# A hybrid decoder step on one core: fifteen of the low parts of the expert rows move from VectorE to GpSimd in each layer

## What is computed

```python
q = (h @ wq).reshape(T, PEER_HEADS, 2, PEER_KDIM // 2)
s = jnp.einsum('thpc,hpkc->thpk', q, subkeys)
s_top, i_top = lax.top_k(s, 16)
cand = s_top[:, :, 0, :, None] + s_top[:, :, 1, None, :]
cs, ci = lax.top_k(cand.reshape(T, PEER_HEADS, 256), 16)
g = jax.nn.softmax(cs, axis=-1)
act = jax.nn.gelu(jnp.einsum('td,thkd->thk', h, u[e]), approximate=False)
out = jnp.einsum('thk,thkd->td', g * act, v[e])
```

## Time and profile before

| What | Value |
|---|---|
| Median of 3 runs | 2259.3 us (2253.72 to 2259.88) |
| Profiled execution: its time | 2260.83 us |
| Its span | 2259.0 us |
| TensorE clock granted, mean | 0.99 |
| Busy: PE, DVE, ACT, POOL | 2180.9, 1562.3, 1281.5, 107.9 us |
| u tiles 0 to 64, first layer | 340 to 535 us of the span |
| u tiles 0 to 64, second layer | 1451 to 1646 us |

### The profile page before, as it was taken

The page is one execution under the profiler, slowest core; times in us unless marked ns, Lnnn a source line. Parts: engine busy times, 40 slices in busy tenths (PEclk is TensorE's granted clock), DMA queues, the critical chain, the costliest instruction groups (busy, mean ns, idle before and its releaser), DMA issues.

```text
span 2259.0 us, 39872 instructions
## 1 busy us (share of the span) xinstructions
PE 2180.9 (97%) x15478; PEld 1844.6 (82%) x15478; DVE 1562.3 (69%) x3318; ACT 1281.5 (57%) x2439; POOL 107.9 (5%) x140
## 2 busy tenths in 40 slices
PE   5999999999999999999999999999999999999998
PEld 3566599999999877778865667999999998777786
DVE  2375469896889877666634754798878897675666
ACT  1254345657888755565513544356588886555654
POOL 1200010000000000000021000100000000001000
PEclk9999999999999999999999999999999999999999
DMA  8342516776565688876563433277765657888564
GB/s 262 135 150 77 201 52 245 263 263 238 199 230 204 230 314 311 309 244 216 178 217 139 145 113 131 100 276 265 256 230 200 227 203 255 310 295 313 186 195 150
DMA packets 143320, 481.67 MB, mean 213 GB/s; under 512 B 25698, under 2 KB 52384, under 8 KB 139022
## 3 DMA queue, kind: packets, MB, share of 16 engines
q1 hardware_dynamic: 132638, 438.71, 56.1%
q0 software_dynamic: 10496, 40.42, 5.0%
HBM read 475.81 MB, written 104.21 MB: 257 GB/s over the span
## 4 chain that ended last, share of the span: by engine, by line
PE 81%; DVE 9%; DMA 6%; SPq 2%; ACT 1%; issue 1%; DVEq 0%; ACTq 0%
PE ps L1140 27%; PE ps L1098 26%; PE ps L806 8%; PE ps L1109 5%; DMA region<-in_peer_v 3%; PE ps L771 3%; DVE parts_low L1976 2%; PE ps L1059 1%; PE ps L1067 1%; PE ps L1063 1%; DMA region<-in_peer_uT 1%; PE ps L796 1%; DMA big<-in_state_win_k 1%; PE ps L815 1%; DVE big L1898 1%
## 5 line engine op out<-in xcount | busy, mean ns | idle before, releaser
L1976 DVE TENSOR_TENSOR parts_low<-region,parts_high 128x1024 fp32r<-128x1024 f32 x512 | 625.7, 1223 | 352.1 <-ACT parts_high L1358 350.3
L1358 ACT CAST parts_high<-region 128x1024 fp32r<-128x1024 f32 x512 | 537.8, 1051 | 307.0 <-PE ps L1140 195.3
L1140 PE MATMUL ps<-parts_high,parts_hw 128*128 128x512 f32 x2048 | 640.0, 392 | 17.3 <-DVE parts_low L1976 11.7
L1098 PE MATMUL ps<-tokens_hi,parts_high 128*128 128x256 f32 x2048 | 590.1, 288 | 14.7 <-DVE parts_low L1976 14.6
L1098 PE MATMUL ps<-tokens_hi,parts_low 128*128 128x256 f32 x2048 | 575.0, 281 | 0.0
L1098 PE MATMUL ps<-parts_hw,parts_high 128*128 128x256 f32 x2048 | 575.0, 281 | 0.0
L1140 PEld LDWEIGHTS ps<-parts_high,parts_hw 128*128 128x128 f32 x2048 | 386.6, 189 | 108.9 <-issue 16.1
L1098 PEld LDWEIGHTS ps<-tokens_hi,parts_high 128*128 128x128 f32 x2048 | 388.1, 190 | 18.8 <-issue 18.0
L1140 PE MATMUL ps<-parts_low,parts_hw 128*128 128x512 f32 x1024 | 400.2, 391 | 0.0
L1098 PEld LDWEIGHTS ps<-parts_hw,parts_high 128*128 128x128 f32 x2048 | 388.0, 189 | 0.0
L1098 PEld LDWEIGHTS ps<-tokens_hi,parts_low 128*128 128x128 f32 x2048 | 387.5, 189 | 0.0
(11 more groups left out here) (300 smaller groups left out, 2290.0 us busy)
## 6 DMA issues: line engine op xcount, KB each, us to landing
region<-in_peer_uT SPq DMA_DIRECT2D x256, 512.0 KB, 4.1
region<-in_peer_v SPq DMA_DIRECT2D x256, 512.0 KB, 4.2
out<-in_state_win_k SPq DMA_DIRECT2D x16, 1536.0 KB, 8.6
out<-in_state_win_v SPq DMA_DIRECT2D x16, 1536.0 KB, 9.0
out<-in_state_win_k SPq DMA_DIRECT2D x16, 1534.5 KB, 8.4
out<-in_state_win_v SPq DMA_DIRECT2D x16, 1534.5 KB, 8.4
big<-in_state_win_k SPq DMA_DIRECT2D x48, 192.0 KB, 3.3
big<-in_state_win_v SPq DMA_DIRECT2D x48, 192.0 KB, 3.6
```

What stands on the lines that cost most here:

```text
L1098: mm = pe.matmul(ps[:, j % ZB, 0:SEQ], a, hp[b][:, c, :], start=(c == 0 and n == 0), stop=(c == KD - 1 and n == 2))
L1140: mm = pe.matmul(ps[:, 2 * half + t, :], wp[j % UN][a][:, 128 * t:128 * t + 128], v_t[b][:, 512 * half:512 * half + 512], start=(j == 0 an ...
L1358: act.copy(hi_t[n % HIGHS], rows_t[n % ROWS]).then_inc(high[l], 1)
L1976: dve.tensor_tensor(lo_t[n % ROWS], rows_t[n % ROWS], hi_t[n % HIGHS], ALU.subtract).then_inc(low[l], 1)
```

## The change

The low parts of the u tiles 7, 11, 15, ..., 63 (`POOL_LOWS`, fifteen in each layer) are subtracted by GpSimd, and VectorE leaves them out. GpSimd counts them on its own semaphore `low_p`, and TensorE waits for that one at these tiles and for `low`, with a count smaller by those left out, at the others (`wait_low`). The DMA of line 737 and the waits around it come into GpSimd's stream between tiles 19 and 23 (`P1_AT`). An unused semaphore goes.

```diff
+POOL_LOWS, P1_AT = range(7, JH, 4), 23
...
+        low_p = sem("row_low_by_gpsimd")
...
+        def wait_low(eng, l, n):
+
+            if n in POOL_LOWS:
+                eng.wait_ge(low_p, POOL_LOWS.index(n) + 1)
+            else:
+                eng.wait_ge(low[l], n + 1 - sum(m <= n for m in POOL_LOWS))
+
...
-                    sp.wait_ge(low[now[0]], 2 * NK - 3)
+                    sp.wait_ge(low[now[0]], 2 * NK - 3 - len(POOL_LOWS))
...
-                pool.wait_ge(p1_ready, 1)
-                pool.dma_start(tq, tpk[64:128, :, :]).then_inc(tq_ld, 16)
-                pool.wait_ge(tq_ld, l * 16 + 16)
-                pool.nop().then_inc(tq_ready, 1)
+
+                def pair_tops():
+                    pool.wait_ge(p1_ready, 1)
+                    pool.dma_start(tq, tpk[64:128, :, :]).then_inc(tq_ld, 16)
+                    pool.wait_ge(tq_ld, l * 16 + 16)
+                    pool.nop().then_inc(tq_ready, 1)
+
+                for n in POOL_LOWS:
+                    if n == P1_AT:
+                        pair_tops()
+                    pool.wait_ge(high[l], n + 1)
+                    pool.tensor_tensor(lo_t[n % ROWS], rows_t[n % ROWS], hi_t[n % HIGHS], ALU.subtract).then_inc(low_p, 1)
+
...
-                    pe.wait_ge(low[l], j + 1)
+                    wait_low(pe, l, j)
...
-                    row_low(j + 2)
+                    if j + 2 not in POOL_LOWS:
+                        row_low(j + 2)
```

More of the change, by code:

```diff
@@ L400, in program @@
         wsel_ready = sem("latent_weights_spread")
-        olT_ready = sem("latent_mix_ready")
         stored = sem("stores_done")
@@ L1136, in y_of @@
                         if half == 0:
-                            pe.wait_ge(low[l], NK + j + 1)
+                            wait_low(pe, l, NK + j)
                         for t in range(2):
```

## The result

The changed kernel takes 2265.2 us (median of 20 runs), the kernel before 2259.3 us (median of 20). The ratio is 1.0027, with a 95% interval of 1.0014 to 1.0039: 6 us slower, between 3 and 9. The forecast was 2263 us, within the bound, with VectorE and GpSimd blocking each other as the likeliest case. The profiled execution has a span of 2264.0 us against 2259.0.

The account below looks back on a forecast made before the run. PE was taken to bound, losing 12.6 us to VectorE. Blocking adds 3.6 us to the profiled 2260.8, giving 2264.4; less 1.5 for that execution's excess over the median, 2263 us. Range 2249 to 2268, likeliest case 2257 to 2268.

Parts of the forecast that it names:

- What bounds: PE bounds; it loses 6.3 us a layer to VectorE around the two `chosen` stretches, 12.6 us in all, the most to gain.
- The blocking: VectorE's two-input instructions and GpSimd's subtractions exclude each other, the later waiting for the whole of the other; chance 0.55.
- The argument from VectorE's copy with one input: One-input copy takes 0.84 ns a column, two inputs 1.19, so two inputs seem to use all fetching, leaving GpSimd none.
- The walk, first place: First `chosen`, tiles 24 to 30: comparison waits 1.6 us, low 30 starts at 429.0 not 427.8, tile 30 1.0 later.
- The walk, second place: Second `chosen`, tiles 51 to 58: low 52 0.6 earlier, a comparison and low 58 each lose 1.1, tile 58 0.5 later.
- Tile 15: High 15 ends late behind its load, so with GpSimd's 2.3 us subtraction the tile is ready 0.3 us late for PE.
- GpSimd's own lateness: PE's waits on GpSimd should be at tiles 15 and 51 only, below 0.5 us.
- The sum: Both places and tile 15 together lose 1.8 us a layer, 3.6 us in all.

Follow-up runs that it names:

- f1_spread: Kernel before, nothing on GpSimd, VectorE's `chosen` steps spread as 12 over 9 u tiles instead of 6: ratio 0.9952 to the kernel before, median 2243.3 us.
- e1_outside: Changed kernel with only tiles 7, 11, 15, 19, 35, 39, 43, 47, 63 on GpSimd, outside VectorE's loaded runs: ratio 1.0000 to the kernel before.
- e3_inside: Changed kernel with only tiles 27, 31, 55, 59 on GpSimd, subtracted during VectorE's `chosen` steps: ratio 1.0021 to the kernel before, median 2263.9 us.
- e2_ahead: Changed kernel with only tiles 23 and 51 on GpSimd, just ahead of VectorE's loaded runs: ratio 0.9992 to the kernel before.
- f2_spread_gp: Changed kernel, fifteen low parts on GpSimd, with the step spreading of f1_spread: ratio 0.9989 to the kernel before, median 2251.6 us.
- e4_reads: Kernel before, VectorE keeps all low parts, GpSimd adds unused subtractions of two constants at tiles 7 to 59: ratio 1.0124 to the kernel before.

## Why the prediction was right

**What bounds.** Right. The loss to VectorE was put at 12.6 us; f1_spread gave back 10.8 (6 to 15), and the yardstick has 11.9 for before and 0.4 for f1_spread.

**The blocking.** Right, and it carries the result. By the Trainium skill, SBUF — State Buffer, section Who interferes with whom, a VectorE instruction with two SBUF inputs and a GpSimd instruction that reads SBUF contend, one that only writes does not, and the later one blocks for the whole of the other; the trace agrees in each point (2.94 us for 1.22 in the changed kernel, 1217 ns beside memsets, 2.88 for 2.46 in the other order). The argument from VectorE's copy with one input, by which the forecast chose its side, was a guess, and no run tests it.

**The walk, first place.** Forecast: the comparison waits 1.6 us, low 30 waits 1.2, tile 30 is 1.0 later. Measured: 1.72 (2.94 - 1.22), 1.25 (2.47 - 1.22), and 1.2 and 1.1 later in the two layers.

**The walk, second place.** Forecast: tile 58 is 0.5 later. Measured: 0.9 and 1.2, of which the later load of tile 51 is 0.2 and 0.4. Without it the place is 0.7 later in both layers. The term is mis-sized by 0.2: low 58 waits 1.2 and not 1.1, and low 52 comes some 0.55 earlier, not 0.6, since the subtraction takes 2.40 us and not 2.3. The comparison waits 1.1 as forecast.

**Tile 15.** Forecast 0.3 us late for GpSimd. Measured from the Gelu of 14 to that of 16, over 5.68 us: 0.95 in the first layer, 0.1 in the second. The view puts the wait down to a Gelu of ScalarE:

```profile
381.73 0.36 PE L1115 MATMUL ps<-tokens_hi,parts_high 128*128 128x256 f32 x1 [0.73 <-ACT big L1428]
```

By the kernel tile 15 waits for the Gelu of tile 11 only, long past, and for its own low part:

```profile
379.19 2.40 POOL L755 TENSOR_TENSOR parts_low<-region,parts_high 128x1024 fp32r<-128x1024 f32 x1 [11.20 <-ACT parts_high L1375]
```

This ends at 381.59, and PE begins 0.14 us later, as it does after GpSimd's low 27 (416.40 and 416.54). So it is GpSimd's lateness. The step that was mis-sized is the load ahead of it: the cast of tile 15 waited 2.06 us for its load here and 1.54 in the kernel before, from which the forecast took its times. In e1_outside, with 1.60 and 1.48, the tile is 0.5 and 0.4 late. Where VectorE makes low 15, waits of 2.6 and 2.7 us for that load make the tile only 0.3 late (e3_inside, e2_ahead).

**GpSimd's own lateness.** Forecast at tiles 15 and 51 only, below 0.5 us. Measured in the first layer at 15, 27, 51 and 55: 0.73, 0.51, 0.54 and 0.20. The last three cost nothing here, because VectorE's later wait absorbs them, but tile 15 lies ahead of all that and costs its full time. In f2_spread_gp, where VectorE is not late, they all count.

**The sum.** Forecast 3.6 us for both layers: 2.0 in the first place, 1.0 in the second, 0.6 at tile 15. Measured in the two traces: 2.2, 2.1 and 1.0, which is 5.3, and the whole stage is 5.4 longer. The medians give 5.9 with an interval of 3 to 9. So the sign and the mechanism were right, and the size came out by a third too small; about half of what is missing is loads that came later in this execution than in that of the kernel before. That the forecast of 2263 lies only 2 us from the measured 2265.2 is no proof of the terms: the measured difference has an interval of 6 us. The waits of single instructions are the proof.

## What to carry to other kernels

In these runs a VectorE instruction with two tensor inputs and a GpSimd instruction that reads SBUF are one resource. Moving a two-input operation from the one to the other makes it 2.40 us long instead of 1.22, and what of it meets a two-input instruction of VectorE is lost again, by VectorE or by GpSimd. It can give something only where VectorE then has one-input work or idle time. At the tiles of e1_outside it mostly has, but there VectorE was not the bound.

Before moving work to another engine, compare the iteration of the loaded engine with that of the engine that bounds (3.53 against 2.84 us here), and look for iterations elsewhere with room: spreading twelve steps over nine tiles gave 10.8 us.

A releaser that a view names is inferred. When it names work that the program doesn't wait for, as at tile 15, the program's waits and the end times say who it was.

## What the runs showed of the hardware

Undisturbed, GpSimd's subtraction of 1024 columns of two float32 tensors takes 2.40 us (2.34 ns a column), its memset of 2048 columns 1.81 us (0.89 ns a column). What was not expected: when GpSimd asks while VectorE is in a two-input instruction and has another one next, either can come out ahead. In e3_inside GpSimd got its turn at the end of the low part, and nearly its whole time fell on the product (3.42 us). In f2_spread_gp it had to let the second addition pass too and was held 1.5 us (3.91 us). The product has a wait on a semaphore of VectorE's own ahead of it and the second addition has none, which may leave GpSimd its turn in the one case and not in the other. In e4_reads GpSimd got in ahead of a product four times more, and at 459.70 it did not get in ahead of a low part, whose wait on `high` was long fulfilled. What decides was not tested.
